# First modulation of a fused two-block network: five of its sixteen columns by matrix products, the opening of the first FFN reordered

## What is computed

```python
mod = (silu(c) @ w_ada + b_ada).reshape(B, 9, D)       # w_ada: 1024 x 9216
m = [mod[:, j] for j in range(9)]
h = rmsnorm(x, ffn1_pre_g) * (1 + m[1]) + m[0]
y = (silu(h @ w_gate) * (h @ w_up)) @ w_down            # D_FF = 2816
x = x + 0.5 * m[2] * rmsnorm(y, ffn1_post_g)
# then the mixer with m[3..5], the second FFN with m[6..8], and two hybrid layers with PEER FFNs
```

## Time and profile before

| | us |
|---|---|
| median of 3 executions | 2512.91 (2509.37 to 2515.11) |
| the profiled execution | 2512.55 |
| its span, first to last instruction | 2510.7 |
| TensorE busy in it | 2432.4 |
| VectorE, ScalarE, GpSimd busy | 1623.3, 1206.1, 697.0 |

### The profile page before, as it was taken

One profiled execution on the slowest core, in us unless ns is written; L12 is line 12 of the kernel. 1 busy time (PEld: TensorE's weight loads), 2 busy tenths in 40 slices (PEclk: granted clock), 3 DMA queues, 4 the chain that ended last, 5 costly groups with the idle time before them and its releaser, 6 DMA issues.

```text
span 2510.7 us, 40330 instructions
## 1 busy us (share of the span) xinstructions
PE 2432.4 (97%) x16355; PEld 2228.2 (89%) x16355; DVE 1623.3 (65%) x3095; ACT 1206.1 (48%) x1827; POOL 697.0 (28%) x333
## 2 busy tenths in 40 slices
PE   4999898999999999999999999999999999999999
PEld 3997888988889999999888888899999999888887
DVE  6887776546575676899544445664676899644444
ACT  4443675445554444443444445655445443444443
POOL 3111001112125661000344443115663000244443
PEclk9999999999999999999999999999999999999999
DMA  7888444655345554444566655435555444555655
GB/s 278 322 303 323 150 140 152 218 193 181 110 146 176 177 178 158 143 137 142 193 195 192 197 190 195 133 129 179 177 173 171 137 141 143 178 196 191 197 191 164
DMA packets 126588, 457.45 MB, mean 182 GB/s; under 512 B 13973, under 2 KB 16961, under 8 KB 125634
## 3 DMA queue, kind: packets, MB, share of 16 engines
q1 hardware_dynamic: 121442, 441.52, 53.1%
q10 hardware_dynamic: 4048, 8.91, 1.1%
q0 software_dynamic: 912, 4.42, 0.5%
HBM read 451.62 MB, written 5.93 MB: 182 GB/s over the span
## 4 chain that ended last, share of the span: by engine, by line
PE 83%; DVE 2%; ACT 1%; issue 0%; POOL 0%; ACTq 0%; POOLq 0%
PE bank L608 25%; PE bank L609 25%; PE bank L610 25%; PE bank L1176 4%; PE bank L956 1%; PE bank L1147 1%; PE bank L817 1%; DVE sb L1852 0%; PE bank L1099 0%; PE bank L623 0%; PE bank L974 0%; POOL sb L2743 0%; DVE sb L1905 0%; PE bank L806 0%; PE bank L1061 0%
## 5 line engine op out<-in xcount | busy, mean ns | idle before, releaser
L608 PE MATMUL bank<-sb,sb 128*128 128x256 f32 (+1 forms) x4744 | 1520.5, 321 | 36.5 <-DVE sb L1852 23.7
L609 PE MATMUL bank<-sb,sb 128*128 128x256 f32 (+1 forms) x4744 | 1494.0, 315 | 0.0
L610 PE MATMUL bank<-sb,sb 128*128 128x256 f32 (+1 forms) x4744 | 1493.9, 315 | 0.0
L1219 ACT ACTIVATE sb<-sb 128x1024 fp32r<-128x1024 f32 x765 | 808.1, 1060 | 1085.2 <-PE bank L610 1077.2
L1852 DVE TENSOR_TENSOR sb<-sb,sb 128x1024 fp32r<-128x1024 f32 x509 | 625.2, 1229 | 585.1 <-ACT sb L1219 583.8
L608 PEld LDWEIGHTS bank<-sb,sb 128*128 128x128 f32 x4744 | 907.9, 191 | 104.6 <-issue 20.9
L2720 POOL TENSOR_TENSOR sb<-sb,sb 128x1024 fp32r<-128x1024 f32 x256 | 629.3, 2460 | 1336.6 <-ACT sb L1219 1332.6
L609 PEld LDWEIGHTS bank<-sb,sb 128*128 128x128 f32 x4744 | 908.9, 192 | 55.0 <-issue 1.0
L610 PEld LDWEIGHTS bank<-sb,sb 128*128 128x128 f32 x4744 | 907.8, 191 | 55.9
L2684 DVE TENSOR_TENSOR sb<-sb,sb 128x1024 fp32r<-128x1024 f32 x64 | 159.9, 2498 | 149.8 <-ACT sb L1808 149.8
L2647 DVE TENSOR_SCALAR sb<-sb,sb 128x128 f32<-128x128 f32 x512 | 142.5, 345 | 0.0
(11 more groups left out here) (272 smaller groups left out, 1193.8 us busy)
## 6 DMA issues: line engine op xcount, KB each, us to landing
sb<-in_peer_down_dram SPq DMA_DIRECT2D x256, 512.0 KB, 3.3
sb<-in_peer_up_dram SPq DMA_DIRECT2D x256, 512.0 KB, 3.3
sb<-in_w_ada_dram SPq DMA_DIRECT2D x72, 512.0 KB, 6.4
sb<-in_hyb_in_dram SPq DMA_DIRECT2D x56, 512.0 KB, 3.4
sb<-in_ffn_gate_dram SPq DMA_DIRECT2D x44, 512.0 KB, 4.2
sb<-in_ffn_up_dram SPq DMA_DIRECT2D x44, 512.0 KB, 4.9
sb<-in_ffn_down_dram SPq DMA_DIRECT2D x44, 512.0 KB, 4.3
sb<-in_mix_in_dram SPq DMA_DIRECT2D x25, 512.0 KB, 3.4
```

Of the source, the lines that this page charges most:

```text
L608: e.matmul(out, a[0], b[0], start=start, stop=False)
L609: e.matmul(out, a[0], b[1], start=False, stop=False)
L610: return e.matmul(out, a[1], b[0], start=False, stop=stop)
L1219: self.e.activation(rr(M.hi[k % NSPLIT]), M.raw[k % NRAW], AF.Copy).then_inc(*self.S.tick("hi", k))
```

## The change

Five columns, n = 0, 1, 4, 8 and 12 (ADA_TENSOR), are computed by TensorE: their tiles are stored transposed in blocks (`columns_T`), silu(c) comes in a second form, as eight columns of 128 (DMA `c_cols`, one small activation), and eight float32 products with one moving column each accumulate a column of `mod` in a bank (`ada_columns`), from which VectorE adds b_ada. The eleven others are VectorE's; GpSimd and ScalarE have no columns any more. The order of tiles goes by pairs of chunks, a modulation covers two chunks instead of four, and VectorE's opening is written out anew (`opening`): sums first, the rests of chunks 0 and 1 after the third modulation, those of 2 to 7 after the fourth. ScalarE writes the high part of a feature itself, as a second activation. TensorE does columns 8 and 12 between the transpositions and tile 0. All sixteen tiles have a buffer of their own, so SP issues them without waiting; x moves from GpSimd's queue to SP's, behind three modulation tiles; tile 0 of the FFN comes before modulation tile 12 instead of 15. The low parts of tiles 1 and 2 move from GpSimd to VectorE. Beside the first FFN SP loads modulation tiles up to eight ahead, into ten buffers.

```diff
 LOWS = {
-    "ffn1": ((1, ("dve",)), (3, ("pool",)), (63, ("dve", "dve", "dve", "dve", "dve", "pool")), (66, ("dve",))),
+    "ffn1": ((3, ("dve",)), (63, ("dve", "dve", "dve", "dve", "dve", "pool")), (66, ("dve",))),
...
-ADA_ORDER = [8 * j + k for k in range(8) for j in (1, 0)] + list(range(16, 72))
+ADA_ORDER = [8 * j + k + i for k in range(0, 8, 2) for j in (0, 1) for i in range(2)] + list(range(16, 72))
-ADA_HALF = 10
+ADA_LATE = 64
-ADA_BESIDE = (1, 4, 6, 11)
+ADA_TENSOR = (0, 1, 4, 8, 12)
...
@@ Tensor.start @@
+        self.ada_columns(0, 2)
+        self.ada_columns(4)
         self.wait_ge("par_in")
         self.wait_ge("con_in")
+
+    def ada_columns(self, first, columns=1):
+        M, e, bank = self.M, self.e, self.take()
+        self.wait_ge("silu_cols")
+        self.K.bank["ada", ADA_ORDER[first]] = bank[:, 0:columns]
+        for i in range(columns):
+            n = first + i
+            w = M.ada[ada_slot(n)]
+            self.wait_ge("ada%d" % ada_slot(n), n)
+            for c in range(8):
+                x = e.matmul(bank[:, i:i + 1], w[:, 128 * c:128 * (c + 1)], M.sc_cols[:, c:c + 1], start=(c == 0), stop=(c == 7))
+            x.then_inc(*self.S.tick("ada_pe", n))
+        self.give(bank, ("mod", 0, ADA_ORDER[first]))
@@ Tensor.ffn @@
         self.features()
+        if self.s == 0:
+            self.ada_columns(8)
+            self.ada_columns(12)
...
@@ Scalar.shifted @@
-        self.e.activation(self.m.f[k % 4], self.turned_chunk("x", k, 4), AF.Identity,
+        for dst in (self.m.f[k % 4],) if s else (self.m.f[k % 4], rr(M.hhi[:, k])):
+            x = self.e.activation(dst, self.turned_chunk("x", k, 4), AF.Identity, scale=M.scales[:, PRE_G[j + 1][1], k:k + 1],
...
@@ Vector @@
+    def opening(self):
+        def rests(*chunks):
+            for k in chunks:
+                self.wait_ge("feature", 0, "x", k)
+                self.e.tensor_tensor(rr(M.hlo[:, k]), f[k % 4], M.hhi[:, k], ALU.subtract).then_inc(*self.S.tick("h_lo", 0, "x", k))
+        self.ada_until(6)
+        self.wait_ge("par_in")
+        self.wait_ge("con_in")
+        for t in range(2):
+            self.root(0, t)
+        self.modulations(0)
+        for t in range(2):
+            self.normalise(0, t)
+        self.ada_until(8)
+        self.modulations(2)
+        self.ada_until(12)
+        self.modulations(4)
+        rests(0, 1)
+        self.split()
+        self.ada_until(16)
+        self.modulations(6)
+        rests(2, 3, 4, 5, 6, 7)
+        self.ahead()
...
@@ Sync.ada_tile @@
+        end = min(n + min(3 + (n - ADA_FIRST) // 4, 8), ADA_LATE + ADA_SLOTS[1]) if n <= ADA_LATE else min(n + 3, len(ADA_ORDER))
+        while self.n_loaded < end:
+            self.ada_load(self.n_loaded)
+            self.n_loaded += 1
...
@@ Sync.start @@
+        self.e.dma_start(self.M.c_cols, self.K.dram["c_cols"]).then_inc(*self.S.tick("c_cols", by=16))
         self.e.dma_start(self.M.c_row[0:1, :], self.K.dram["c"]).then_inc(*self.S.tick("c_in", by=16))
+        for n in range(ADA_FIRST):
+            if n == 3:
+                x = self.K.dram["x"].rearrange("b (t p) d -> p b t d", p=128)[:, 0]
+                self.e.dma_start(self.M.x, x).then_inc(*self.S.tick("x_in", by=16))
+            if n == 12:
+                self.load(0)
             self.ada_load(n)
```

140 lines of the change are left out of this document (57 added, 83 removed).

## The result

The changed kernel takes 2494.41 us (median of 4, 2493.02 to 2497.01) beside 2512.80 us for the kernel before (4 runs, 2509.37 to 2515.11): a ratio of 0.9929 with a 95% interval of 0.9912 to 0.9946, a gain of 18.4 us where 11.5 were forecast. A second comparison, made later, gave 0.9949 (0.9933 to 0.9965), medians 2496.34 and 2510.91; one execution of 4833.58 us among its five counts in that median and is left out of the ratio. The mean of all ten other executions of the changed kernel in this study is 2495.5, that of the 23 of the kernel before 2511.6, so all of them together give a gain of **16.1 us**.

A forecast was written before the change was run, and what follows sets the result against it. The prediction took VectorE's late work in the opening, stretched beside wide GpSimd operations, as the bound on TensorE's dense start. 2512.9 minus 11.5 (opening gain, 0 later) gave 2501.4 us, with 8 in 10 in 2496.5 to 2508.

The forecast's parts named there:

- The opening: Kernel start up to TensorE's dense run: VectorE's shorter path starts it at 33.0 instead of 46.06; gain 11.5 us.
- closing remark: VectorE's opening: a modulation step dearer than 0.6 us most cheaply breaks the forecast, as four lie on the path.
- Landings: Opening transfers: modulation tile 5 lands at 15.5, the last at 29.2, FFN tiles 0 and 1 at 24.2 and 30.5.
- Columns: TensorE's five columns in the opening: at most 4.3 us each, estimate 1.7, path cost 0 (range 0 to 0.7).
- ScalarE: Opening: second activations, 0.48 us each, hide behind VectorE's sums except the last two; rest 7 ends near 35.4.
- Rival 1: Opening: columns and early chunks raise TensorE's clock sooner; gain 12.6 us, time 2500.3; chance 0.12.
- Rival 2: First FFN: five additional modulation loads delay FFN tiles, giving back 6.25 us; gain 5.2, time 2507.7; chance 0.15.
- Rival 3: Opening not shortened: SP's queue runs dry or VectorE stays stretched without GpSimd; gain about 3, time 2510; chance 0.10.
- Rival 4: Opening: TensorE's columns are expensive, up to 0.945 us a piece, and delay the last modulation; time 2521; chance 0.03.
- Later: FFN behind the opening: deeper modulation loading taken as 0, bounds +1 to -6.25 us; the rest slides as a whole.
- The spread: Whole time: runs vary some 3 us to either side; 8 in 10 lie in 2496.5 to 2508.

The follow-up runs named there:

- experiment 3: Kernel before, with VectorE doing all sixteen sums and the low parts of tiles 1 and 2, so nothing wide on GpSimd in the opening: 2508.94 us.
- late_rests: Changed kernel with the first two rests and the low part of tile 0 put behind the fourth modulation on VectorE: 2495.35 us.
- after: First profile of the changed kernel, nothing edited; that kernel's median of 4 is 2494.41 us.
- after_third: Changed kernel profiled again, nothing edited: 2496.34 us (median of five).
- look3: Changed kernel with SP's modulation loads beside the first FFN three tiles ahead instead of up to eight, ring of four buffers not started at once: 2499.14 us.
- ring4: Changed kernel with modulation tiles beside the first FFN loaded as before the change, three ahead and into four buffers: 2494.31 us.

## Why the prediction was right or wrong

**The opening: right in mechanism, 1.1 us too small.** Forecast 11.5 with 10 to 12.1 as its range, measured 12.6. The bound was VectorE, the stretched operations were due to GpSimd (experiment 3), and behind them the path runs through 8 sums, 3 modulations, 2 rests and a low part as set out. Three terms were each a little dear, and the first of the four modulations was rightly hidden behind GpSimd, so the prediction's closing remark that all four are on the path is not so. The start: the sum of tile 5 begins at 15.24 instead of 15.5 and the normalisations end at 18.92 instead of 19.4, 0.5. A modulation takes 0.46 us (21.21 to 21.67), not 0.6, 0.4 for the three behind. The two rests take 0.67 from start to start (25.57 to 26.24), not 0.86, 0.2. Fourth modulation at 31.27 against 32.4, dense run at 31.74 against 33.0, high part 3 at 36.0 (mean) against 37.3, high part 4 at 40.1 against 41.5.

**Landings: right.** Tile 5 was put at 15.5, the last modulation tile at 29.2, FFN tiles 0 and 1 at 24.2 and 30.5; they came at 15.22, 29.42, 24.30 and 30.70. The sentence that the transfers are no limit was true for the forecast's 32.4 and no longer quite for 31.27 (late_rests).

**Columns: right that they are hidden, too dear by a fifth.** 3.5 us at 1.2 GHz (14.03 to 17.6) against the transpositions' 4.3 as upper bound, and 1.84 us in the one that ran at 2.4 GHz. The Trainium skill ("TensorE: Matmul & The Clock Gate", LDWEIGHTS) has a weight load cost its columns over 1.2, in ns, and the estimate from it was 1.7 us a column. The trace disagrees: at 1.2 GHz a column takes 3.5 us, twice that, and even at 2.4 GHz 1.84. Column 8 was ready before it was asked for, and column 12 at 29.1 to 29.3 before 30.81.

**ScalarE: right.** Eight activations in 3.76 us, high part 0 at 24.32; only rest 7 waited for it (0.48).

**Rival 1, an earlier clock: not what happened, though its 12.6 is the number measured.** That is luck: the 12.6 come from VectorE being 1.1 us earlier. In after, behind columns and transpositions, the granted clock was full at 21.1, half again from 24.5 to 34.8, and rose 2.95 us into the dense run, four products before tile 0's end. In after_third the first rise comes only at 37.15, behind the end of tile 0. From the dense start to high part 3 the one takes 3.83 us and the other 4.31, so this rise is worth 0.5. Chunks 2 to 7 run without a wait in either, 0.21 us apart at 1.2 GHz, and rest 7 is done at 34.12 while its products start at 34.96: TensorE's own pace sets that stretch. What a rise at its start would bring, no run shows. It is in the text that behind a hole before chunk 2 the clock may be low again, and it was.

**Rival 2: fell** (look3, ring4: no effect). **Rival 3: fell**: SP's queue held all transfers, DMA share 1.03 from 20 to 28.2. **Rival 4: fell**, 0.22 us a piece.

**"Later", taken as 0: this is the step that failed.** The bounds were a gain of 1 and a loss of 6.25 (five loads of 1.25 us); the measured gain of 3.2 lies outside them, on the side that was given almost nothing. The 0 rested on "every wait is for work that slides too". That is not so for a wait whose end is a landing: a write that is issued at the same point of the schedule landed after 5.7 to 7.0 us in the kernel before and after 4.4 to 4.7 in the changed one, and with it came or went a held GpSimd, a late FFN tile 15 and a longer wait at the gate row. The earlier trace rows shows two of these waits, 2.55 and 3.48 us, and the prediction took them for the place where extra loads might hurt, not for time that could come back. In the changed kernel they are 0.14 to 0.99 and 1.75. Of the 3.2, 2.2 are shown to belong to this task by moving it; 1.0 is the meeting at tile 29. Why the write lands sooner in the changed kernel stays open.

**The spread.** 2.6 of the 6.9 us between the forecast's gain and the measured one lie neither in the opening nor in the FFN up to high part 48. The forecast gave "some 3 us to either side" for runs, about what half-rate stretches cost, and set the lower end, 2496.5, 4.9 below its centre. The opening's 1.1 and the 3.2 of "Later" take 4.3 of that, and one absent fall passes it. Both terms were outside their own bounds (12.1 and 1), and "Later" is the one without which the time would have been inside.
